# Layer 0's shift and scale in two halves of the model dimension, and a new order for the first weight units

## What is computed

```python
mod = c_act @ ada_w[i] + ada_b[i]
sh1, sc1, g1, sh2, sc2, g2 = jnp.split(mod[:, None, :], 6, axis=-1)
h = rms_norm(x, norm_mix[i]) * (1.0 + sc1) + sh1
qkv = h @ w_qkv        # layer 0: three head groups, q, k and v of 8 heads each
```

## Time and profile before

| | us |
|---|---|
| time, median of 3 runs (lowest, highest) | 910.11 (909.47, 910.36) |
| span of the profiled execution, which is its own time from first to last instruction | 910.1 |
| PE busy | 847.7 (93%) |
| DVE busy | 623.6 (69%) |
| ACT busy | 426.3 (47%) |
| GpSimd busy | 119.3 (13%) |
| first multiply of unit 0 starts | 42.47 |
| unit 9, the first of pair 1, starts | 99.76 |

### The profile page before, as it was taken

One profiled execution on the slowest core, in us unless ns is written; L12 is line 12 of the kernel. 1 busy time (PEld: TensorE's weight loads), 2 busy tenths in 40 slices (PEclk: granted clock), 3 DMA queues, 4 the chain that ended last, 5 costly groups with the idle time before them and its releaser, 6 DMA issues.

```text
span 910.1 us, 10752 instructions
## 1 busy us (share of the span) xinstructions
PE 847.7 (93%) x4195; PEld 709.3 (78%) x4195; DVE 623.6 (69%) x749; ACT 426.3 (47%) x515; POOL 119.3 (13%) x159
## 2 busy tenths in 40 slices
PE   1599999999999979999999979999989799999997
PEld 0477888889888858888888857888877588888886
DVE  5879678677686767766777775895774754454543
ACT  3255446545455355333433446658554553433431
POOL 4101001010010010111111100462620000000000
PEclk9999999999999999999999979999979899999999
DMA  9899766876767627889889835444224175555541
GB/s 339 284 271 310 240 224 214 274 222 231 230 221 243 190 89 249 286 277 316 283 278 318 294 109 182 139 139 139 93 93 139 46 225 191 185 185 185 185 139 46
DMA packets 119607, 188.96 MB, mean 208 GB/s; under 512 B 5580, under 2 KB 90758, under 8 KB 119558
## 3 DMA queue, kind: packets, MB, share of 16 engines
q1 hardware_dynamic: 105350, 137.90, 47.4%
q0 software_dynamic: 14208, 50.39, 15.9%
HBM read 187.18 MB, written 1.09 MB: 207 GB/s over the span
## 4 chain that ended last, share of the span: by engine, by line
PE 81%; DVE 8%; DMA 4%; ACT 3%; issue 2%; SPq 2%; DVEq 0%; ACTq 0%
PE bank L390 69%; PE bank L659 2%; PE bank L508 2%; PE bank L484 2%; DMA raw<-in_attn_w_qkv_dram 1%; DVE wlo L1052 1%; PE bank L469 1%; PE bank L604 1%; ACT arena L774 1%; PE bank L434 1%; SPq L268 1%; PE bank L406 1%; DMA arena<-in_distance_table_dram 1%; DMA bias_rows<-arena 1%; DMA ada_w<-in_ada_w_dram 1%
## 5 line engine op out<-in xcount | busy, mean ns | idle before, releaser
L1052 DVE TENSOR_TENSOR wlo<-raw,whi 128x2048 fp32r<-128x2048 f32 x126 | 288.7, 2291 | 126.6 <-ACT whi L724 126.3
L390 PE MATMUL bank<-whi,hT_hi 128*128 128x512 f32 (+1 forms) x800 | 315.7, 395 | 8.7 <-DVE hT_lo L1145 8.3
L724 ACT ACTIVATE whi<-raw 128x2048 fp32r<-128x2048 f32 x126 | 241.5, 1916 | 150.3 <-PE bank L390 120.5
L390 PE MATMUL bank<-whi,hT_lo 128*128 128x512 f32 (+1 forms) x800 | 308.5, 386 | 0.0
L390 PE MATMUL bank<-wlo,hT_hi 128*128 128x512 f32 (+1 forms) x800 | 308.0, 385 | 0.0
L390 PEld LDWEIGHTS bank<-whi,hT_hi 128*128 128x128 f32 x800 | 152.7, 191 | 42.6 <-DVE hT_lo L1145 10.1
L390 PEld LDWEIGHTS bank<-whi,hT_lo 128*128 128x128 f32 x800 | 152.4, 191 | 30.4
L390 PEld LDWEIGHTS bank<-wlo,hT_hi 128*128 128x128 f32 x800 | 152.8, 191 | 28.8 <-issue 1.0
L1077 DVE SCALAR_TENSOR_TENSOR acc<-ada_w,cact,acc 128x1024 f32<-128x1024 f32 x80 | 102.3, 1279 | 25.0 <-DMA ada_w<-in_ada_w_dram 24.6
L390 PE MATMUL bank<-whi,oT_hi 128*128 128x512 f32 x240 | 97.4, 406 | 3.6 <-DVE oT_lo L1430 1.6
L312 POOL DMA_DIRECT2D ada_w<-in_ada_w_dram x80 | 42.6, 532 | 408.3 <-DVE acc L1077 408.3
(11 more groups left out here) (137 smaller groups left out, 734.0 us busy)
## 6 DMA issues: line engine op xcount, KB each, us to landing
raw<-in_ffn_w_dram SPq DMA_DIRECT2D x88, 512.0 KB, 4.9
ada_w<-in_ada_w_dram POOLq DMA_DIRECT2D x80, 512.0 KB, 5.2
raw<-in_attn_w_qkv_dram SPq DMA_DIRECT2D x64, 512.0 KB, 4.8
raw<-in_ffn_w_dram SPq DMA_DIRECT2D x22, 1024.0 KB, 6.0
raw<-in_hgrn_w_in_dram SPq DMA_DIRECT2D x16, 1024.0 KB, 5.4
arena<-in_ada_w_dram POOLq DMA_DIRECT2D x16, 512.0 KB, 6.6
raw<-in_attn_w_qkv_dram SPq DMA_DIRECT2D x4, 1024.0 KB, 5.1
raw<-in_attn_w_out_dram SPq DMA_DIRECT2D x4, 1024.0 KB, 6.0
```

The source lines that it names most:

```text
L390: mm = nc.tensor.matmul(d[:, 0:n], l, r[:, k, cut], start=first and k == 0 and q == 0, stop=last and k == nk - 1 and q == 2)
L724: return nc.scalar.activation(dst, src, ACT.Copy)
L1052: nc.vector.tensor_tensor(wlo[:, m % SPL, :], raw[:, m % RAW, :], fp(whi[:, m % SPL, :]), ALU.subtract).then_inc(s["split"], 1)
```

## The change

The columns of `ada_w` that layer 0's first shift and scale need are cut in another way: block 0 is now the shift and the scale of features 0 to 511, block 1 those of features 512 to 1023 (`halves`). After block 0 and its reduction, half of h can be made. PE works with it on three first halves of chunks: the order of pair 0's units becomes 0, 2, 4, 1, 3, 5, 6, 7, 8 (`ORDER0`), and chunk 2 gets banks 4 and 5 of PSUM. Beside that:

- A tile of blocks 0 and 1 is one DVE operation of 1024 columns, not two of 512; its transfer takes two pieces of 2 KB from each row of `ada_w`, not one of 4 KB.
- `c` is loaded first on SP and transposed alone; GpSimd issues its first two tiles before it makes the identity and without a wait for the clearing of `acc`.
- x is scaled by ACT, and the raw transposes are copied out by ACT into `hT`; scale and shift are then applied in place, two slices on DVE and two on ACT (`first_affine`, `first_round`).
- The bias table is copied by ACT before it scales x.
- Unit 0 is loaded when `ada_used` is 5, units 1 and 2 when it is 8, the point from which GpSimd loads block 1's tiles too.
- The masks load after unit 20, the two first biases after unit 6. The `ada_op`s of later blocks start at unit 3 and catch up: two of them at units 3, 14 and 25.
- The sigmoid of the recurrence's lower bound moves into layer 1.

```diff
+ORDER0 = (0, 2, 4, 1, 3, 5, 6, 7, 8)
...
@@ sync
             for m in range(UNITS):
-                if m == 0:
-                    sp.wait_ge(s["ada_used"], KC)
+                if m < 2:
+                    sp.wait_ge(s["ada_used"], (5, KC)[m])
...
                 if m == 2:
-                    sp.dma_start(masks[:], a["pair_masks"]).then_inc(s["masks_in"], 16)
                     sp.wait_ge(s["tab_cp"], 1)
                     sp.dma_start(scratch, tabT).then_inc(s["tab_out"], 16)
+                if m == 6:
                     sp.wait_ge(s["tab_out"], 16)
+                    sp.wait_ge(s["ada_used"], 2 * KC)
                     load_bias(sp, 0)
                     load_bias(sp, 1)
...
@@ gpsimd
                 if n < 2 * KC:
                     if n >= FIRST:
-                        pool.wait_ge(s["ada_used"], n - FIRST + 1)
+                        pool.wait_ge(s["ada_used"], KC if n == FIRST else n - FIRST + 1)
...
@@ tensor
-            for r in range(3):
-                reduce_task(r, 3 if r < 2 else 2)
+            reduce_task(0, 3)
+            half_unit(0, 0, (0, 1))
             pe.wait_ge(s["tab_cp"], 1)
+            half_unit(1, 0, (0, 1))
+            pe.wait_ge(s["h0_raw"], 4)
+            half_unit(2, 0, (0,))
+            reduce_task(1)
+            half_unit(2, 0, (1,))
...
@@ vector
+def halves(v, blk):
+    return v.rearrange("p (w h c) -> p w h c", w=ADA_BLOCKS, h=2)[:, 0:2, blk, :]
...
+def ada_done(m):
+    return -(-max(0, m - 2) * PAIRS * QU // (PAIRS * QU - 3))
```

More of the change, by code:

```diff
@@ L351, in hybrid_trunk, with qk_bank, qk_sets, qk_last @@
         LATE = 4 * (PAIRS - 1)
+        def qk_bank(n, which):
+            return bank[7] if n < 3 and which else bank[6]
+        def qk_sets(m):
+            pr, j = divmod(m, QU)
+            if pr == 0:
+                return [(j - 5, which) for which in range(2)] if 5 <= j <= 7 else []
+            return [(3 * pr + (j - 3) // 2, (j - 3) % 2)] if pr < PAIRS and 3 <= j <= 8 else []
+        def qk_last(m):
+            pr, j = divmod(m, QU)
+            first = 3 if pr == 0 else 1
+            step = 1 if pr == 0 else 2
+            n, odd = divmod(j - first, step)
+            return 3 * pr + n if pr < PAIRS and odd == 0 and 0 <= n < 3 else None
         def second(J):
@@ L522, in qkv_extra @@
                         att_transposes(J)
-                if pr < PAIRS and 3 <= j <= 8:
-                    qk_transposes(3 * pr + (j - 3) // 2, (j - 3) % 2)
-            first_units(0, 0, [[bank[0]], [bank[1]]])
-            for m in range(PURE):
-                if m >= 2:
-                    qkv_unit(m)
+                for n, which in qk_sets(m):
+                    qk_transposes(n, which)
+            for m in range(3, PURE):
+                qkv_unit(m)
                 qkv_extra(m)
@@ L790, in _, with first_round @@
                 norm_stats(0, t)
+            act.wait_ge(s["tab_mm"], 1)
+            copy(tabT, bank[2][0:GH, 0:TABLE]).then_inc(s["tab_cp"], 1)
+            act.wait_ge(s["newton"], 3)
+            for t in range(T):
+                nc.scalar.activation(xn[:, t], x[:, t], ACT.Copy, scale=small[:, 2 + t:3 + t]).then_inc(s["xn_s"], 1)
+            for t in range(T):
+                for g in range(2):
+                    act.wait_ge(s["xn_tr"], 2 * t + g + 1)
+                    copy(hT[:, 4 * g:4 * g + 4, t * P:(t + 1) * P],
+                         bank[4 + 2 * t + g][:].rearrange("p (k t) -> p k t", k=4)).then_inc(s["h0_raw"], 1)
+            def first_round(half, t):
+                cut = slice(t * P, (t + 1) * P)
+                first = 4 * half + 2
+                for kc in range(first, 4 * half + 4):
+                    i = nc.scalar.activation(hT[:, kc, cut], hT[:, kc, cut], ACT.Identity, bias=mod_b[:, 0, 0, kc:kc + 1],
+                                             scale=mod_a[:, 0, 0, kc:kc + 1])
+                i.then_inc(s["h0_aff_s"], 1)
+                act.wait_ge(s["h0_aff_s"], 2 * half + t + 1)
+                act.wait_ge(s["h0_aff"], 2 * half + t + 1)
+                copy(hT_hi[:, 4 * half:4 * half + 4, cut], hT[:, 4 * half:4 * half + 4, cut]).then_inc(s["xn_hi"], 1)
             round_unit(0)
-            norm_round(0, 0)
+            act.wait_ge(s["h0_raw"], 4)
+            act.wait_ge(s["ada_ev"], 1)
+            first_round(0, 0)
+            first_round(0, 1)
             round_unit(1)
-            norm_round(0, 1)
+            round_unit(2)
+            act.wait_ge(s["ada_ev"], 2)
+            first_round(1, 0)
+            first_round(1, 1)
             def qk_square(n):
@@ L1188, in _, with first_rest @@
+            def first_rest(half, t):
+                dve.wait_ge(s["xn_hi"], 2 * half + t + 1)
+                v = lambda y: y[:, 4 * half:4 * half + 4, t * P:(t + 1) * P]
+                nc.vector.tensor_tensor(v(hT_lo), v(hT), fp(v(hT_hi)), ALU.subtract).then_inc(s["xn_lo"], 1)
+            for blk in range(2):
+                nc.vector.memset(acc[:, blk], 0.0).then_inc(s["ada_zero"], 1)
             dve.wait_ge(s["cact_s"], 1)
-            dve.wait_ge(s["ada_zero"], 1)
-            for n in range(2 * KC):
+            for n in range(KC):
@@ new lines, in _ @@
+            first_affine(0, 1)
+            first_rest(0, 0)
+            first_rest(0, 1)
+            ada_op(KC)
+            split_unit(1)
+            for n in range(KC + 1, KC + 4):
+                ada_op(n)
+            split_unit(2)
+            for n in range(KC + 4, 2 * KC):
+                ada_op(n)
+            ada_evac(1)
+            dve.wait_ge(s["ada_ev"], 2)
+            first_affine(1, 0)
+            first_affine(1, 1)
+            first_rest(1, 0)
+            first_rest(1, 1)
```

238 lines of the change are left out of this document (130 added, 108 removed).

## The result

The change takes 922.5 us (median of 4 runs, 920.34 to 923.78) against 909.79 before: ratio 1.0136, 95% interval 1.0119 to 1.0154. By that ratio it is slower by 12.4 us (by the two medians 12.7), where 5.1 less was forecast. The profiled execution has a span of 922.0 (before: 910.1), 11.9 more. The difference is all made by 119 us: unit 9, at 99.76 before, starts at 109.50, 9.7 later, and a new pause of 2.58 us follows behind it, 12.3 together. The pauses of PE farther on are those of before, shifted, and none differs by more than 0.8 us.

What follows compares the result with a forecast made beforehand. PE nearly always has work past the start, so the gain is how much earlier than 99.76 unit 9 starts: 53.9 + 22.3 + 18.5 = 94.7, 5.1 earlier, so 910.1 - 5.1 = 905.0 us; range 902.0 to 909.0.

Steps and rivals of the forecast that it cites:

- Branch (a), the table: Before unit 0's rounding: PE reads the bias table at 14 (bounds 13.2 and 16); after ACT's copies, rounding ends at 23.7.
- Branch (b): Data before unit 0's rounding: DVE's eighth sum by 19, unit 0 issued at about 15, landed at 20, rounded at 22.
- S+16.05 ... a tie: From first multiply S (28.6): DVE's sums and splits end S+16.05, PE arrives S+16.0; unit 3 at S+25.3 = 53.9.
- The reduction is half of the 16 columns: PE's second reduction before unit 3: half of the 16 columns that took 3.57, so 1.8 us, ending at S+17.9.
- The clock: PE's clock falls in the 4.7 us pause before unit 3: about ten multiplies at 0.2 more, 2.0 us on unit 3.
- It falls twice: Rival: PE's clock falls before unit 6 too, 2 us more, 907.0; chance 0.14 for this or the late table alone.
- To unit 6, 22.3: Unit 3 to unit 6: DVE's splits, sums, reductions, normalisations and waits for ACT, 22.2 (22.3 in the sum); PE pauses for 3.
- masks and biases free: Moved loads: the masks behind unit 20 counted as free, covered by three loaded units; no cost entered for the moved biases.
- To unit 9, 18.5: Unit 6 to unit 9: units 6, 7 and 8 and four sets of transposes, 18.5 us, so unit 9 at 94.7.
- Nothing changed after it: Sign of being right: nothing changes behind unit 9; the doubled sums at units 14 and 25 cost nothing.
- supply sets it: Rival: at 239 GB/s the last tile comes at 51.7, unit 3 at 62.2, unit 9 at 103: 913.4; chance 0.09.
- The rule weighed: Round robin by packet would let the small bias table pass sooner, 903.6 not 905.0; set aside, as a rival chance 0.12.

Runs made afterwards that it cites:

- row_first: The change with the first block's 4 KB bias row issued on POOL ahead of the eight tiles, not behind the third: 919.53 us, ratio 1.0116 to the kernel before.
- units_early: The change with SP asking for units 0, 1 and 2 one after the other once three sums are done: 914.97 us, ratio 1.0062 to the kernel before.
- split2_behind: The change with all eight sums of block 1 before unit 2's split, and the second reduction before unit 2: 914.05 us, ratio 1.0061 to the kernel before.
- rows_later: The change with the reductions of blocks 2 and 3 behind units 10 and 12, not 9 and 10: 917.6 us, ratio 1.0096 to the kernel before.
- the seven edits: The change with earlier unit requests, unit 2's split behind the sums, later reductions, bias row first, later biases, two reorderings of units 3 to 8's sums: 904.76 us, ratio 0.9958.
- third_queue: The change with unit 2's two pieces issued by ACT once the eighth sum is done, not by SP: 919.82 us, ratio 1.0104 to the kernel before.

## Why the prediction was wrong

- *Branch (a), the table:* right. PE read it at 13.33 (forecast 14, before 13.22), with the new packets of the tiles beside it. Behind it the branch was late: ACT's scaling of x waited for DVE until 17.13 (forecast 16.1), and its last copy ended at 22.65 (21.8). It hid behind branch (b), since the rounding waited for unit 0 until 23.59.
- *Branch (b), "DVE's eighth sum ends by 19" and unit 0 "issued at about 15":* wrong by 3.6 and 3.4. The sums began at 10.92, behind a bias row that GpSimd issues behind three tiles. I had moved that row with the code and put its cost at nothing. The first multiply came at 30.62, not 28.6; row_first gives 28.89.
- *"S+16.05 ... a tie", and so unit 3 at S+25.3:* the step that failed. It was S+32.7. The sum counted DVE's and PE's work and no arrival. Unit 2 was asked for at 24 and landed at 42.9. Its split was due when DVE had done three of the sums, at 39.13, which is S+8.5 (in units_early it starts at S+8.5 without a wait), and it started 5.78 later. That is most of the 7.4; nearly all the rest is the second reduction, 1.4 longer than in the sum. units_early (25.7) and split2_behind (24.4) show that the rest of the step was sized right.
- *"The reduction is half of the 16 columns":* a misreading. The 16 instructions of the earlier trace rows are 8 columns, two instructions each, and the second reduction of the change is 16 instructions too: 3.2 us here, at the lower clock, and 1.9 where PE was at the higher. The forecast's 1.8 was near only to the second.
- *The clock:* forecast 2.0 on unit 3. It cost 1.6 there (7.1 for 5.5), some 3 more on unit 6 (8.58 for 5.48) and 1.3 on the second reduction (3.2 for 1.9). "It falls twice", before unit 6 too, was right as a mechanism and priced at 2; it fell a third time, before the second reduction.
- *To unit 6, 22.3:* 24.6. The biases behind unit 6 cost 2.1 of it (22.5 without); "masks and biases free" was wrong for the biases, with unit 7 and a tile of the ring behind them, and for the masks nothing in the trace speaks against it.
- *To unit 9, 18.5:* 21.55, the 3 of the clock.
- *"Nothing changed after it":* wrong by 2.58. I checked the doubled sums at units 14 and 25, not that block 2's eighth sum must be done when unit 9 is; rows_later shows it.

The steps' errors add up: 2.0 + 7.4 + 2.3 + 3.05 + 2.6 = 17.35, and 905.0 + 17.35 = 922.35. With the causes cleared by the seven edits, unit 9 stands at 93.43, 1.3 before the forecast 94.7, and the median at 904.76. That this meets the forecast 905.0 is luck: two of the edits move sums that the forecast had ahead of unit 6, and of the 6.3 won at unit 9 only 4.6 is left in the span.

- *The rival "supply sets it"* had the right sign and the wrong place. It asked for the last tile (GpSimd's, decided from 48.5 on), and the tiles were in time. The last was SP's unit, at 380 GB/s in all: the rival reckoned with one rate for all requests and not with the part of each queue. That DVE then waits for `wlo`'s input, not for `ada_w`, wasn't among my signs.
- *The rule weighed.* The Trainium skill (DMA: Bandwidth & Descriptors, Queues, rings and completion order) has each DMA engine go round robin between queues by packet. I used it for a small table, where it changed nothing. It bears on the units, and there the trace agrees, if a packet of the profile is what the Trainium skill calls one: wherever two or three queues had transfers waiting, each got the same number of packets (1094 and 1092 from 30 to 42.9 us; 306, 305 and 304 in third_queue). By such turns 1 KB against 3.5 KB is 22% of 383 GB/s, 84, and 84 is what SP got. The 119 and 109 further up are averages over stretches in which one of the queues had nothing to move for a while. The rule that I set aside gives, put to the units, the term that the sum lacked: of the 2.24 MB 0.88 had come by 28 us, and the other 1.36 at 84 GB/s would end at 44.2 (an estimate from these rows), near the 42.9 measured.

## What to carry to other kernels

An earlier start is worth nothing until the arrival of everything behind it is in the sum: write down for each load when it is asked for, on which queue, beside which backlog, and when it is due. A queue's part of the DMA engines went by packets here, so a load in rows of 1 KB beside a backlog in packets of 3.5 KB got 22% of the bytes; whether the same units in longer rows would land sooner wasn't tried. In an engine's queue, put an operation whose input may be late behind the ones whose inputs are there and which others wait for. Work tied to a step number (a sum at unit 9, a reduction behind unit 9) must be checked again when the steps before it move against it.
